# Gated-delta heads: decay rows by DMA a head ahead, key lengths from the Gram diagonal, output squares summed in one product

## The chip, the core and the metric

The kernel runs on one core of one Trainium2 chip. A core has five engines that run side by side and meet through semaphores: TensorE (PE in the profile; PEld is its weight load), VectorE (DVE), ScalarE (ACT), GpSimd (POOL) and SyncE (SP), which here only issues DMAs. SBUF is the on-chip memory with 128 partitions; PSUM (8 banks of 512 fp32 columns) is where TensorE writes. The metric is the device time of one execution in microseconds (us). The time before is 3914.38 us, the median of 3 runs (3914.11 to 3916.15).

## The reference, cut to what matters

The model is a chain of four blocks (attention, Hyena, gated DeltaNet with experts, short convolution with experts) on 512 tokens of width 1024, with 256 context tokens. The change touches only the DeltaNet mixer, which has 8 heads of width 128 and runs in two directions ("lanes"):

```python
qkv = silu(conv3_seq(p[..., :3 * d], conv_w))
q = l2norm(q) * HEAD_DIM ** -0.5        # l2norm(t) = t * rsqrt(sum(t * t) + 1e-6)
k = l2norm(k)
beta = sigmoid(...)                     # per token, direction, head
g = -exp(a_log) * softplus(a_in + dt_bias)
# gated_delta_scan, for each chunk, direction and head
gc = cumsum(g)
decay = exp(where(incl, gc[:, None] - gc[None, :], -inf))
lmat = where(i > j, (k * beta) @ k.T * decay, 0)
sol = triangular_solve(lmat, [v * beta, k * beta * exp(gc)])     # u, w
v_new = u - w @ s
s_next = s * exp(gc[-1]) + (k * exp(gc[-1] - gc)).T @ v_new
o = (q * exp(gc)) @ s + (q @ k.T * decay) @ v_new
# afterwards, per token and head
o = o * rsqrt(mean(o * o) + 1e-6) * onorm
y = (o * silu(z)) @ w_out
```

## The kernel before, in words

Every stage is a class with one method for each engine (`tensor`, `vector`, `scalar`, `gpsimd`, `sync`), and the order of the instructions on an engine is the order in which these methods issue them. Nothing is reordered; an engine that waits holds up all that stands behind it. `DeltaHeads` is one stage. It works in chunks of 128 tokens: `NTA` = 6 chunks (2 of context, 4 of latent tokens, `KEYS` = 768 columns), and for each of the 8 heads there are two parts.

*The inversion* (`tensor_invert`, `vector_invert`, `scalar_invert`) builds the inverse of the triangular matrix by doubling, in levels v = 1 to 6, for both lanes. A level is `masked(v, l)` on TensorE (L2498, 24 fp32 matmuls of 64x64 a lane), `keep_masked` on VectorE (L2838), `update(v, l)` on TensorE (L2519), `turn` on VectorE (L2844, a transpose from PSUM) and `keep_update` on ScalarE (L2698). The next level's `masked(v+1, l)` waits for `turn(v, l)`; `update(v, l)` waits for `keep_masked(v, l)` and for the `keep_update` of the level before. In the gaps TensorE does work that isn't part of the chain: it turns values and keys (L2442, L2448), sums the squares of the output of the head before (`tensor_sums`, L2457 and L2458, after level 3), spreads the root over the partitions (`tensor_spread`, L2465, after level 4), and computes the decay rows of the next head's lane 0 (`decays`, L2412, in level 5). An fp32 matmul leaves two MATMUL records; fp32r matmuls (L588) leave one.

*The scan* (`tensor_scan` and so on) walks through the 6 chunks of both lanes in steps 0 to 5. In each step TensorE multiplies the state by the keys (L2554, z), VectorE forms r (L2874), TensorE multiplies by the inverse (L2568, vn), ScalarE scales (L2742), VectorE scales again (L2884, vnd), TensorE makes the state's update (L2591, su) and VectorE adds it (L2893, s). Between these stand the projections of the *next* head (`project`, L588, three fp32r matmuls for each of 8 pieces), which are most of the work of the scan; ScalarE and VectorE convolve and activate the next head's q, k, v beside them. Step 0 ends with the decay rows of lane 1 of the next head (L2412), which wait until ScalarE has read those of lane 0 out of the same two PSUM banks (`grown`, L2645). Step 3 has the next head's Gram matrix k'k (L2423) and, behind it, the key lengths: ScalarE squares k into SBUF (L2633), and 6 matmuls against a column of ones sum the squares (L2427); VectorE waits for them (L2768) in `column_scales`.

The decay rows of a lane are a matrix whose every partition holds the cumulated g of all 768 tokens. `decay` on ScalarE makes of them exp(-relu(...)) in `L_M` (6 pieces by L2641, then L2644) and exp of the row in `L_KBG` (L2645). GpSimd halves them (L2220), and in `pool_head`, at the start of the inversion, reads `L_KBG` for the last columns (L2230), for q times decay (L2234), and makes q'k times decay (L2237); then it multiplies the gate by the head's output (L2245) and splits the next head's weights into a high and a low part (L582), each of which waits for ScalarE's copy of the high part (L577), which waits for the DMA of the weights.

SyncE issues four DMAs of 512 KB for the next head's weights as soon as the projections of the head before have ended (L2311). Counted semaphores: `COUNTED` gives names to certain counts of one semaphore.

The output of a head is normed in the inversion of the next head: ScalarE keeps it and squares it (L2678, L2682), TensorE sums the squares of o with those of q (times an epsilon), ScalarE takes the root (L2687), VectorE inverts it (L2822), TensorE spreads it, and VectorE multiplies (`norm_o`, L2829).

Of the kernel before, what the change touches and what calls it, by code (L numbers as in the profile page):

```python
# [1956 lines left out]
class DeltaGates:  # L1957
# [3 lines left out]
    def __init__(self, core):  # L1961
        self.c = core
        self.n = core.slab(k_slab(core.d["w_in_a_2"][0], 4 * D, 4 * D + 32))
        self.rows, self.rows0 = core.shared("table_in", 48)
# [168 lines left out]
class DeltaHeads(Stage):  # L2133
# [13 lines left out]
    PER = {"slab": 64, "full": 6, "centre": 5, "conv": 5, "silu": 6, "square": 1, "coef": 1, "nk": 1,  # L2147
           "osq": 1, "ostd": 1, "oroot": 1, "weighed": 1, "mixed": 1, "values_out": 1, "keys_out": 1, "qk": 1,
           "tri": 2, "cross": 2, "side": 1, "scored": 1, "a": 12, "a_in": 10, "a_out": 14, "x": 12,
           "upd": 12, "z": 10, "r": 10, "vn": 12, "vn_out": 13, "vnd": 12, "su": 12, "s": 12, "o": 1,  # L2150
           "begun": 7, "grew": 5, "onorm": 2}


    COUNTED = {"rows": ("begun", (1, 2)), "gram": ("begun", (3,)), "lens": ("begun", (4,)), "qkp": ("begun", (5,)),
               "turned": ("begun", (6, 7)), "flat": ("grew", (1, 3)), "grown": ("grew", (2, 4)), "eg": ("grew", (5,)),
               "osum": ("onorm", (1,)), "ospread": ("onorm", (2,))}

    def __init__(self, core, gates):
# [11 lines left out]
        self.sums, self.inverse, self.nk, self.root = (v(G_COL + 72 + 6 * i, n) for i, n in enumerate((NTA, NTA, NTA, NT)))  # L2170
# [33 lines left out]
    def gpsimd(self, pool):  # L2204
        for h in range(DHEADS):
            if h == 0:
                self.weights_low(pool, 0)
            self.halve_decays(pool, h)
            self.pool_head(pool, h)
            if h + 1 < DHEADS:  # L2210
                self.weights_low(pool, h + 1)
        self.weigh_o(pool, DHEADS - 1)
# [9 lines left out]
    def pool_head(self, pool, h):  # L2222

        if h:
            self.wait(pool, h - 1, "o", 1)
            self.wait(pool, h - 1, "s", 12)
# [12 lines left out]
        if h:  # L2239
            self.weigh_o(pool, h - 1)  # L2240

# [57 lines left out]
    def sync(self, sp):  # L2299
# [15 lines left out]
    def tensor(self, pe):  # L2315
        self.project(pe, 0, 1, range(KD))
# [5 lines left out]
        self.decays(pe, 0, 0)  # L2322
        self.decays(pe, 0, 1)
# [6 lines left out]
        self.tensor_spread(pe, DHEADS - 1)  # L2330

    def vector(self, dve):
# [18 lines left out]
        for h in range(DHEADS):  # L2351
            self.vector_invert(dve, h)
            self.vector_scan(dve, h)
        self.invert_root(dve, DHEADS - 1)
        self.norm_o(dve, DHEADS - 1)

    def scalar(self, act):
# [8 lines left out]
        self.square_k(act, 0)  # L2366
        self.centre(act, 0, 4)
        self.silu(act, 0, 3)
        self.silu(act, 0, 4)
        self.gate(act, 0)  # L2370
# [31 lines left out]
    def decays(self, pe, h, l):  # L2402

        c = self.c
        if l == 1:
            self.wait(pe, h, "grown", 1)
        elif h:
            self.wait(pe, h - 1, "keys_out", 1)
        else:
            pe.wait_ge(self.cols, 1)  # L2410
        for t in range(NTA):
            ins = pe.matmul(c.pair(6, KEYS)[:, P * t:P * t + P], self.g_all[:, t, l, h:h + 1].to_broadcast([P, P]),  # L2412
                            c.const(("cum_f", "cum_b")[l]), start=True, stop=True)
        ins.then_inc(self.s["begun"], 1)

    def gram(self, pe, h):
# [3 lines left out]
        self.wait(pe, h, "grown", 2)  # L2420
# [8 lines left out]
        ins.then_inc(self.s["begun"], 1)  # L2429

    def scores(self, pe, h):
        c = self.c
        self.wait(pe, h, "silu", 3)
        for t in range(NTC, NTA):
# [16 lines left out]
    def tensor_sums(self, pe, h):  # L2451

        c = self.c
        self.wait(pe, h, "osq", 1)
        for t in range(NT):
            out, cols = c.ps[:, 5, TC + t:TC + t + 1], slice(P * t, P * t + P)
            pe.matmul(out, self.o_sq[:, cols], c.const("one_over_p")[:, 0:1], start=True, stop=False)  # L2457
            ins = pe.matmul(out, self.q_sq[:, cols], c.eps(4), start=False, stop=True)  # L2458
        ins.then_inc(self.s["onorm"], 1)

    def tensor_spread(self, pe, h):
        c = self.c
        self.wait(pe, h, "oroot", 1)
        for t in range(NT):
            ins = pe.matmul(c.ps[:, 5, P * t:P * t + P], self.root[:, t:t + 1].to_broadcast([P, P]),  # L2465
                            c.const("ident"), start=True, stop=True)
        ins.then_inc(self.s["onorm"], 1)

    def tensor_invert(self, pe, h):
# [13 lines left out]
        def masked(v, l):  # L2483
# [5 lines left out]
            elif h and l == 0:  # L2489
                self.wait(pe, h - 1, "s", 12)  # L2490
# [38 lines left out]
        for v in range(2, LEVELS):  # L2529
# [4 lines left out]
            if v == 5 and h + 1 < DHEADS:  # L2534
                self.decays(pe, h + 1, 0)
# [4 lines left out]
            if v == 4 and h:  # L2540
                self.tensor_spread(pe, h - 1)

    def tensor_scan(self, pe, h):
        c, s = self.c, self.s
        more = h + 1 < DHEADS
        for step in range(NTA):
# [27 lines left out]
            for l in range(2):  # L2574
# [56 lines left out]
    def square_k(self, act, h):  # L2631
        act.drain()
# [1260 lines left out]
```

## Time and profile before

| | |
|---|---|
| time before, median of 3 | 3914.38 us |
| the profiled execution's own time | 3914.16 us |
| its span | 3912.3 us |
| TensorE busy | 3454.4 us (88% of the span) |
| VectorE busy | 1812.2 us (46%) |
| ScalarE busy | 1110.1 us (28%) |
| GpSimd busy | 420.5 us (11%) |
| `DeltaHeads`, first to last head's inversion | 1838 to 2370 us |

The lines of a timeline are: start, duration, engine, line of the kernel, operation, output and input by memory area, shape, count; in square brackets the idle time ahead of it on that engine and what ended it. Several like instructions in a row are merged. Matmuls overlap: the distance of two starts tells what one takes of the engine, not the duration.

### The profile page before, as it was taken

How to read it: one execution, taken by the hardware profiler on the slowest of the kernel's cores; microseconds unless marked ns; L12 is line 12 of the kernel's file. 1: busy time of each engine (PE TensorE's matmuls, PEld its weight loads, DVE VectorE, ACT ScalarE, POOL GpSimd, SP SyncE). 2: the span in 40 equal slices, each digit the busy share in tenths (PEclk: the TensorE clock that was granted, in tenths of full speed). 3: DMA queues.
4: the chain of work that ended last, by engine and by line, in shares of the span. 5: the costliest groups of instructions: out<-in, count | busy, mean ns of one | idle time of the engine just before them, and what ended most of it. 6: DMA issues, size and time to landing. Idle time of an engine off the chain costs nothing. (4 is left out here: it accounts for less than half of the span.)

```text
span 3912.3 us, 48632 instructions
## 1 busy us (share of the span) xinstructions
PE 3454.4 (88%) x18766; PEld 2323.2 (59%) x18766; DVE 1812.2 (46%) x2892; ACT 1110.1 (28%) x1849; POOL 420.5 (11%) x420
## 2 busy tenths in 40 slices
PE   8999899878999899887999998699987896998886
PEld 6756577754756677755888887444332674443332
DVE  6773777447865777435455445411111543111112
ACT  3051433223201433235544453211111322111112
POOL 1200000000300000002222320011111000111110
PEclk7999999988999899998999998799999897999998
DMA  6430355320622255310001001299997413999995
GB/s 220 172 109 22 107 173 172 114 108 22 247 108 86 86 172 172 109 26 23 23 23 45 23 23 46 98 414 392 424 415 300 167 45 118 417 402 415 398 391 218
DMA packets 222472, 689.48 MB, mean 176 GB/s; under 512 B 27699, under 2 KB 107699, under 8 KB 197076
## 3 DMA queue, kind: packets, MB, share of 16 engines
q1 hardware_dynamic: 192000, 648.17, 43.2%
q10 hardware_dynamic: 11572, 21.96, 1.5%
q0 software_dynamic: 18720, 16.84, 1.3%
q8 instruction: 126, 2.06, 0.2%
q14 instruction: 54, 0.44, 0.0%
HBM read 697.38 MB, written 40.89 MB: 189 GB/s over the span
## 5 line engine op out<-in xcount | busy, mean ns | idle before, releaser
L588 PE MATMUL psum<-work_rounded 128*128 128x512 f32 (+1 forms) x2224 | 815.4, 407 | 80.3 <-DVE work_rounded L582 30.3
L588 PE MATMUL psum<-work_rounded,ring_rounded 128*128 128x512 f32 (+1 forms) x1824 | 726.1, 398 | 0.0
L588 PEld LDWEIGHTS psum<-work_rounded 128*128 128x128 f32 x2224 | 428.7, 193 | 203.0 <-issue 93.9
L3434 PE MATMUL psum<-ring,fixed 128*64 128x512 f32 x1184 | 415.8, 657 | 96.1 <-DMA ring<-in_w 52.9
L577 ACT ACTIVATE work_rounded<-ring 128x1024 fp32r<-128x1024 f32 x204 | 214.6, 1057 | 950.7 <-PE psum L588 692.7
L588 PE MATMUL psum<-fixed_rounded,work_rounded 128*128 128x512 f32 (+1 forms) x1088 | 435.9, 401 | 0.0
L588 PEld LDWEIGHTS psum<-work_rounded,ring_rounded 128*128 128x128 f32 x1824 | 352.6, 193 | 81.1
L3589 DVE TENSOR_TENSOR work<-work,psum 64x512 f32<-64x512 f32 (+1 forms) x64 | 44.2, 691 | 701.9 <-ACT work L3519 547.3
L582 DVE TENSOR_TENSOR ring_rounded<-ring,work_rounded 128x1024 fp32r<-128x1024 f32 x189 | 230.1, 1220 | 283.0 <-ACT work_rounded L577 283.0
L3434 PEld LDWEIGHTS psum<-ring,fixed 128*64 128x64 f32 x1184 | 131.7, 150 | 333.0 <-issue 333.0
L362 DVE SCALAR_TENSOR_TENSOR work<-ring,fixed,work 128x512 f32<-128x512 f32 x364 | 300.5, 835 | 24.8 <-issue 0.9
L3434 PE MATMUL psum<-work,fixed 128*64 128x512 f32 x512 | 240.8, 626 | 0.0
L588 PE MATMUL psum<-ring_rounded 128*128 128x512 f32 (+1 forms) x768 | 238.5, 372 | 0.3 <-issue 0.3
L588 PEld LDWEIGHTS psum<-fixed_rounded,work_rounded 128*128 128x128 f32 x1088 | 210.7, 194 | 46.6 <-issue 2.6
L1274 DVE SCALAR_TENSOR_TENSOR work<-psum,fixed,work 128x511 f32<-128x511 f32 (+1 forms) x152 | 109.4, 720 | 142.1 <-ACT work L1356 108.2
L3519 ACT ACTIVATE work<-psum 64x512 f32<-64x512 f32 x53 | 31.3, 590 | 477.5 <-PE psum L3434 477.5
L3422 PE MATMUL psum<-ring,fixed 128*128 128x512 f32 x352 | 158.9, 611 | 1.8 <-DVE fixed L3581 1.8
L3343 POOL DMA_INDIRECT pair_rows<-work x66 | 66.7, 1011 | 809.0 <-DVE work L3605 663.8
L582 POOL TENSOR_TENSOR ring_rounded<-ring,ring_rounded 128x1024 fp32r<-128x1024 f32 x32 | 76.7, 2410 | 715.8 <-ACT ring_rounded L577 715.8
L588 PEld LDWEIGHTS psum<-ring_rounded 128*128 128x128 f32 x768 | 139.2, 189 | 21.1 <-issue 1.6
L582 POOL TENSOR_TENSOR ring_rounded<-ring,fixed_rounded 128x1024 fp32r<-128x1024 f32 x23 | 48.6, 2115 | 873.3 <-ACT fixed_rounded L577 873.3
L588 PE MATMUL psum<-fixed_rounded,ring_rounded 128*128 128x512 f32 (+1 forms) x384 | 137.0, 357 | 0.0
(396 smaller groups left out, 5159.7 us busy)
## 6 DMA issues: line engine op xcount, KB each, us to landing
ring<-in_w SPq DMA_DIRECT2D x128, 2048.0 KB, 17.3
work<-in_w SPq DMA_DIRECT2D x64, 2048.0 KB, 21.5
ring<-in_mod_w SPq DMA_DIRECT2D x24, 2048.0 KB, 9.0
ring<-in_ada_w SPq DMA_DIRECT2D x24, 2048.0 KB, 7.9
ring<-in_ffn_w_in SPq DMA_DIRECT2D x44, 1024.0 KB, 7.6
ring<-in_ffn_w_out SPq DMA_DIRECT2D x10, 2048.0 KB, 7.7
ring<-in_w_in_a SPq DMA_DIRECT2D x32, 512.0 KB, 6.6
ring<-in_hy_w_in SPq DMA_DIRECT2D x6, 2048.0 KB, 8.2
```

Of the source, the lines that this page charges most:

```text
L362: ins = dve.scalar_tensor_tensor(out=acc, in0=w[:, k, :], scalar=c.par(cond, k), in1=acc, op0=ALU.mult, op1=ALU.add)
L577: return act.activation(c.rounded(out), v, ACT.Copy)
L582: return eng.tensor_tensor(c.rounded(v), v, c.rounded(v_high), ALU.subtract)
L588: ins = pe.matmul(out, c.rounded(w), c.rounded(x), start=(start and i == 0), stop=(stop and i == 2))
L1274: dve.scalar_tensor_tensor(out=out[:, 1:n], in0=u[:, 0:n - 1], scalar=w0, in1=out[:, 1:n], op0=ALU.mult, op1=ALU.add)
L3343: pool.indirect_dma_start(self.c.d["pair_rows"], bass.IndirectOffsetOnAxis(ap=self.si[:, b:b + 1].bitcast(U32), axis=0), self.y_sb[:, b, : ...
L3422: ins = pe.matmul(c.ps[:, 2 + j, :], self.gt_sb[:, k, :], weights(o, j)[:, k, :], start=(k == 0), stop=(k == KD - 1))
L3434: ins = pe.matmul(c.ps[64 * j:64 * j + 64, 2, :], self.gt_sb[:, k, 0:64], weights(o, j)[:, k, :], start=(k == 0), stop=(k == KD - 1))
L3519: act.activation(self.s_sb[64:P, :].rearrange("p (k q) -> p k q", k=4), by_row(c.ps[0:64, 2, :]), ACT.Silu)\
L3589: dve.tensor_tensor(hh, s_sb, by_row(c.ps[rows, bank, :]), ALU.mult).then_inc(self.prod, 1)
```

## The change

- The decay rows come from memory. In head 0 the cumulated sums of all heads (96 columns) are transposed once on TensorE, copied by ScalarE and written to a table in DRAM (`keep_table`, DMA issued by ScalarE). From then on SyncE fetches both lanes' rows for the next head with two DMAs, broadcast to all partitions, straight into `L_KBG` of each lane, as soon as GpSimd has read the old ones (`scored`). ScalarE reads them there and writes the exp over them. TensorE's `decays` are left for head 0 only.
- The key lengths are the diagonal of the Gram matrix: VectorE multiplies its two 64-row halves by the identity and reduces. ScalarE's squares of k and TensorE's 6 products go.
- The output's squares: ScalarE scales q's square, GpSimd adds it to that of o (`add_q`, now the first thing in `pool_head`), and one 128x512 product against a matrix of 1/128 sums them. VectorE transposes the sums in 32x32 blocks (`turn_o`, level 4), ScalarE takes the root of 16 columns, and VectorE inverts and spreads it with a block transpose (`invert_root`, moved to level 5). `tensor_spread` goes.
- The state isn't updated any more in the last step of the scan, where nobody reads it.

```diff
     def pool_head(self, pool, h):
         if h:
+            self.add_q(pool, h - 1)
             self.wait(pool, h - 1, "o", 1)
-            self.wait(pool, h - 1, "s", 12)
+            self.wait(pool, h - 1, "s", 10)
...
+        if h == 0:
+            pool.wait_ge(self.gates.rows, self.gates.rows0 + 64)
...
+    def add_q(self, pool, h):
+        self.wait(pool, h, "osq", 1)
+        pool.tensor_tensor(self.o_sq, self.o_sq, self.q_sq, ALU.add).then_inc(self.s["ofull"], 1)
...
     def sync(self, sp):
...
+            if h == 0:
+                sp.wait_ge(self.gates.rows, self.gates.rows0 + 64)
+                continue
+            self.wait(sp, h - 1, "scored", 1)
+            for l in range(2):
+                rows = self.table.rearrange("(t l) (b n) -> l b t n", l=2, n=P)[l, h]
+                sp.dma_start(self.lane(l, L_KBG, NTA, P), rows.partition_broadcast(P)).then_inc(self.s["rows"], 16)
...
     def tensor(self, pe):
...
-        self.decays(pe, 0, 0)
-        self.decays(pe, 0, 1)
+        pe.wait_ge(self.cols, 1)
+        pe.transpose(c.ps[0:96, 3, 0:P], c.view(G_GC, 96), c.const("ident")).then_inc(self.gates.turned, 1)
+        self.first_decays(pe, 0)
+        self.first_decays(pe, 1)
...
     def gram(self, pe, h):
         self.wait(pe, h, "silu", 2)
-        self.wait(pe, h, "grown", 2)
+        if h == 0:
+            self.wait(pe, 0, "grown", 2)
         for t in range(NTA):
             ...
-        self.wait(pe, h, "square", 1)
-        for t in range(NTA):
-            ins = pe.matmul(c.ps[:, 7, TC + t:TC + t + 1], self.lane(0, L_L, NTA, P)[:, t, :],
-                            c.const("ones")[:, 0:1], start=True, stop=True)
...
     def tensor_sums(self, pe, h):
-        self.wait(pe, h, "osq", 1)
-        for t in range(NT):
-            out, cols = c.ps[:, 5, TC + t:TC + t + 1], slice(P * t, P * t + P)
-            pe.matmul(out, self.o_sq[:, cols], c.const("one_over_p")[:, 0:1], start=True, stop=False)
-            ins = pe.matmul(out, self.q_sq[:, cols], c.eps(4), start=False, stop=True)
-    def tensor_spread(self, pe, h):
...
+        self.wait(pe, h, "ofull", 1)
+        pe.matmul(c.ps[:, 5, :], c.const("one_over_p"), self.o_sq, start=True, stop=True).then_inc(self.s["osum"], 1)
...
     def tensor_invert(self, pe, h):
...
-            if v == 5 and h + 1 < DHEADS:
-                self.decays(pe, h + 1, 0)
...
-            if v == 4 and h:
-                self.tensor_spread(pe, h - 1)
     def tensor_scan(self, pe, h):
...
-                self.wait(pe, h, "vnd", i + 1)
-                pe.matmul(c.ps[:, 2 * l, 2 * P:3 * P], self.kt[:, t, :], self.st(l, 3), start=True, stop=True)\
-                    .then_inc(s["su"], 1)
+                if step < NTA - 1:
+                    self.wait(pe, h, "vnd", i + 1)
+                    pe.matmul(c.ps[:, 2 * l, 2 * P:3 * P], self.kt[:, t, :], self.st(l, 3), start=True, stop=True)\
+                        .then_inc(s["su"], 1)
...
-                if step == 0:
-                    self.decays(pe, h + 1, 1)
...
+    def keep_table(self, act):
+        act.wait_ge(self.gates.turned, 3)
+        staged = self.lane(0, L_QD, P)[0:96, :]
+        act.activation(staged, self.c.ps[0:96, 3, 0:P], ACT.Copy).then_inc(self.cols, 1)
+        act.wait_ge(self.cols, 2)
+        act.dma_start(self.table.rearrange("a (b n) -> (a b) n", n=P), staged).then_inc(self.gates.rows, 16)
...
     def decay(self, act, h, l):
-        m, rows = self.lane(l, L_M, NTA, P), c.pair(6, KEYS).rearrange("p (t n) -> p t n", n=P)
-        self.wait(act, h, "rows", l + 1)
+        m, rows = self.lane(l, L_M, NTA, P), self.lane(l, L_KBG, NTA, P)
+        if h:
+            self.wait(act, h - 1, "rows", 32)
+        else:
+            act.wait_ge(self.gates.turned, 4 + l)
+            rows = c.pair(6, KEYS).rearrange("p (t n) -> p t n", n=P)
...
     def column_scales(self, dve, h):
-        self.wait(dve, h, "lens", 1)
-        dve.tensor_scalar(self.sums, self.c.ps[:, 7, TC:TC + NTA], RMS_EPS, None, ALU.add)
+        self.wait(dve, h, "gram", 1)
+        g, diagonal = self.c.pair(6, KEYS).rearrange("p (t n) -> p t n", n=P), self.compact(0, L_L)
+        for half in self.halves():
+            dve.tensor_tensor(diagonal[half], g[half, :, half], self.ident()[half], ALU.mult)
+        dve.drain()
+        dve.tensor_reduce(self.sums, diagonal, AX.X, ALU.add)
+        dve.drain()
+        dve.tensor_scalar(self.sums, self.sums, RMS_EPS, None, ALU.add)
...
+    def turn_o(self, dve, h):
+        self.wait(dve, h, "osum", 1)
+        dve.transpose(self.o_sq, self.c.ps[:, 5, :])
+        dve.drain().then_inc(self.s["oturn"], 1)
     def invert_root(self, dve, h):
         self.wait(dve, h, "ostd", 1)
         dve.reciprocal(self.root, self.root)
-        dve.drain().then_inc(self.s["oroot"], 1)
+        dve.drain()
+        spread(dve, self.o_sq, self.root)
+        dve.drain()
     def norm_o(self, dve, h):
-        self.wait(dve, h, "ospread", 1)
         self.wait(dve, h, "weighed", 1)
-        dve.scalar_tensor_tensor(..., in1=self.c.ps[:, 5, :], ...)
+        dve.scalar_tensor_tensor(..., in1=self.o_sq, ...)
     def vector_invert(self, dve, h):
         for v in range(1, WHOLE + 1):
...
+            if v == 4 and h:
+                self.turn_o(dve, h - 1)
+            if v == WHOLE and h:
+                self.invert_root(dve, h - 1)
             for l in range(2):
                 turn(v, l)
...
-            if v == 4 and h:
-                self.invert_root(dve, h - 1)
     def vector_scan(self, dve, h):
...
+                if step == NTA - 1:
+                    continue
```

The `continue` stands in both inner loops of `vector_scan` (vnd and s). ScalarE's `deviate_o` (the root) moves from level 3 to level 4, ahead of `square_q`, and `square_o` waits for the norm of the head before.

## Rows read from the trace of the kernel before

**Rows 1.** Window of one head: length, busy us (instructions) of each engine, PEclk.
```profile
2064.91:2141.09 76.18, 72.58 (x896) 64.66 (x897) 39.32 (x90) 36.55 (x78) 21.04 (x16) 1.00 0.12 29
```
**Rows 2.** Timeline of TensorE in the scan: end of step 0, then steps 3 and 4.
```profile
2102.13 1.60 PE L2412 MATMUL psum<-fixed,work 128*128 128x128 f32 x12 [0.29 <-ACT work L2645]
2103.57 0.61 PE L2554 MATMUL psum<-work 128*128 128x128 f32 x4
...
2119.17 1.40 PE L2427 MATMUL psum<-fixed,work 128*128 128x1 f32 x12
2120.43 0.36 PE L588 MATMUL psum<-ring_rounded 128*128 128x256 f32 x1
...
2125.84 0.75 PE L2568 MATMUL psum<-work 128*128 128x128 f32 x4
```
**Rows 3.** Timeline of ScalarE, first instruction of steps 1 and 2.
```profile
2105.16 0.62 ACT L2742 ACTIVATE work<-psum,work 128x128 f32<-128x128 f32 x2 [3.08 <-PE psum L2568]
...
2110.68 0.62 ACT L2742 ACTIVATE work<-psum,work 128x128 f32<-128x128 f32 x2 [1.06 <-PE psum L2568]
```
**Rows 4.** Timeline of VectorE, steps 3 and 4 of the same scan.
```profile
2123.39 0.16 DVE L2768 TENSOR_SCALAR work<-psum 128x6 f32<-128x6 f32 x1
...
2124.24 1.12 DVE L2782 TENSOR_TENSOR work<-work,psum 64x384 f32<-64x384 f32 x2 [0.19 <-issue]
2125.43 0.61 DVE L2874 SCALAR_TENSOR_TENSOR work<-psum,work 128x128 f32<-128x128 f32 x2
```
**Rows 5.** Groups of VectorE by form: busy us, mean ns of one, then idle.
```profile
L1113 DVE TENSOR_REDUCE work<-psum 128x1 f32<-128x768 f32 x32 | 29.1, 952 | 12.3 <-PE psum L1070 12.3
...
L512 DVE STREAM_TRANSPOSE work<-psum 128x512 f32<-128x512 f32 x11 | 7.9, 716 | 37.5 <-PE psum L478 37.5
```
**Rows 6.** Timelines at a change of heads: VectorE, TensorE and GpSimd.
```profile
1908.39 0.75 DVE L1277 SCALAR_TENSOR_TENSOR work<-psum,fixed,work 128x511 f32<-128x511 f32 x1
...
1910.26 0.55 DVE L2793 TENSOR_TENSOR work<-work 128x384 f32<-128x384 f32 x1
...
1912.85 1.15 DVE L2795 TENSOR_TENSOR work<-work 128x384 f32<-128x384 f32 x1
...
1914.73 0.86 PE L2480 MATMUL psum<-work,fixed 64*64 64x384 f32 x4 [0.86 <-DVEq L2798]
...
1912.76 0.82 POOL L2231 COPY work<-work 128x768 f32<-128x768 f32 x1
```
**Rows 7.** Timelines of VectorE and GpSimd in levels 3 and 4.
```profile
2079.80 1.41 DVE L2815 COPY work<-work 128x6 f32<-128x6 f32 x2
...
2082.02 1.26 DVE L2838 TENSOR_TENSOR work<-psum,work 128x384 f32<-128x384 f32 x2 [0.65 <-PE psum L2498]
...
2076.45 4.67 POOL L582 TENSOR_TENSOR ring_rounded<-ring,ring_rounded 128x1024 fp32r<-128x1024 f32 x2 [3.31 <-ACT ring_rounded L577]
```
**Rows 8.** Timeline of TensorE, the sums, then levels 4 and 5.
```profile
2079.18 0.38 PE L2457 MATMUL psum<-fixed,work 128*128 128x1 f32 x2
...
2081.06 1.61 PE L2498 MATMUL psum<-work 64*64 64x64 f32 x48
...
2086.11 1.61 PE L2498 MATMUL psum<-work 64*64 64x64 f32 x48
```
**Rows 9.** The DMA issues: KB of each, median us to landing.
```profile
ring<-in_w_in_a SPq DMA_DIRECT2D x32, 512.0 KB, 6.6
```
**Rows 10.** Windows with PEclk: the first head's opening, then two in the experts.
```profile
1813.00:1843.60 30.60, 16.91 (x122) 14.49 (x122) 8.86 (x17) 10.47 (x22) 9.59 (x9) 0.61 0.28 70
...
2813.00:2816.40 3.40, 3.40 (x10) 1.20 (x8) 0.00 (x0) 0.00 (x0) 1.24 (x2) 0.50 1.00 423
...
2864.20:2891.00 26.80, 21.84 (x109) 8.75 (x105) 4.13 (x6) 4.76 (x8) 3.66 (x6) 1.00 1.01 425
```
**Rows 11.** Timeline of TensorE, two matmuls of the experts behind idle time.
```profile
2811.83 0.61 PE L3434 MATMUL psum<-ring,fixed 128*64 128x512 f32 x1 [2.00 <-DMA work<-in_w]
...
2875.75 0.61 PE L3434 MATMUL psum<-ring,fixed 128*64 128x512 f32 x1 [2.00 <-DMA work<-in_w]
```

More of the change, by code:

```diff
@@ L1963, in __init__ @@
         self.n = core.slab(k_slab(core.d["w_in_a_2"][0], 4 * D, 4 * D + 32))
-        self.rows, self.rows0 = core.shared("table_in", 48)
+        self.rows, self.rows0 = core.shared("table_in", 64)
         (self.full, self.sigmoid, self.shifted, self.soft, self.gate, self.turned) = (
@@ L2133 @@
 class DeltaHeads(Stage):
-    PER = {"slab": 64, "full": 6, "centre": 5, "conv": 5, "silu": 6, "square": 1, "coef": 1, "nk": 1,
-           "osq": 1, "ostd": 1, "oroot": 1, "weighed": 1, "mixed": 1, "values_out": 1, "keys_out": 1, "qk": 1,
+    PER = {"slab": 64, "full": 6, "centre": 5, "conv": 5, "silu": 6, "coef": 1, "nk": 1, "rows": 32,
+           "osq": 1, "ofull": 1, "oturn": 1, "ostd": 1, "weighed": 1, "mixed": 1, "values_out": 1, "keys_out": 1, "qk": 1,
            "tri": 2, "cross": 2, "side": 1, "scored": 1, "a": 12, "a_in": 10, "a_out": 14, "x": 12,
[L2150 to L2156, printed above, removed]
+           "upd": 12, "z": 10, "r": 10, "vn": 12, "vn_out": 13, "vnd": 10, "su": 10, "s": 10, "o": 1,
+           "begun": 4, "grew": 5, "osum": 1}
+    COUNTED = {"gram": ("begun", (1,)), "qkp": ("begun", (2,)), "turned": ("begun", (3, 4)),
+               "flat": ("grew", (1, 3)), "grown": ("grew", (2, 4)), "eg": ("grew", (5,))}
     def __init__(self, core, gates):
@@ L2169, in __init__ @@
         self.kd, self.gl, self.eg, self.bg, self.coef, self.ahead = (v(G_COL + 12 * i, 2, NTA) for i in range(6))
-        self.sums, self.inverse, self.nk, self.root = (v(G_COL + 72 + 6 * i, n) for i, n in enumerate((NTA, NTA, NTA, NT)))
+        self.sums, self.inverse, self.nk, self.root = (v(G_COL + 72 + 6 * i, n) for i, n in enumerate((NTA, NTA, NTA, T // 32)))
+        self.table = core.d["h_rows"][0:2 * NTA, :]
         self.taps = v(PAR0 + PAR["conv_a0"][0], 3, 3, DHEADS)
@@ L2211, in gpsimd @@
                 self.weights_low(pool, h + 1)
+        self.add_q(pool, DHEADS - 1)
         self.weigh_o(pool, DHEADS - 1)
@@ L2353, in vector @@
             self.vector_scan(dve, h)
+        self.turn_o(dve, DHEADS - 1)
         self.invert_root(dve, DHEADS - 1)
@@ L2369, in scalar @@
         self.silu(act, 0, 4)
+        self.keep_table(act)
         self.gate(act, 0)
@@ L2400, in project, with first_decays @@
             ins.then_inc(self.s["full"], 1)
-    def decays(self, pe, h, l):
+    def first_decays(self, pe, l):
         c = self.c
[L2405 to L2410, printed above, removed]
+        if l:
+            self.wait(pe, 0, "grown", 1)
         for t in range(NTA):
-            ins = pe.matmul(c.pair(6, KEYS)[:, P * t:P * t + P], self.g_all[:, t, l, h:h + 1].to_broadcast([P, P]),
+            ins = pe.matmul(c.pair(6, KEYS)[:, P * t:P * t + P], self.g_all[:, t, l, 0:1].to_broadcast([P, P]),
                             c.const(("cum_f", "cum_b")[l]), start=True, stop=True)
-        ins.then_inc(self.s["begun"], 1)
+        ins.then_inc(self.gates.turned, 1)
     def gram(self, pe, h):
@@ L2433, in scores @@
         self.wait(pe, h, "silu", 3)
+        if h == 0:
+            pe.wait_ge(self.cols, 2)
         for t in range(NTC, NTA):
@@ L2489, in masked @@
             elif h and l == 0:
-                self.wait(pe, h - 1, "s", 12)
+                self.wait(pe, h - 1, "s", 10)
             if v > WHOLE:
@@ L2629, in convolve @@
             .then_inc(self.s["conv"], 1)
-    def square_k(self, act, h):
-        act.drain()
-        act.activation(self.lane(0, L_L, KEYS), self.k, ACT.Square).then_inc(self.s["square"], 1)
+    def keep_table(self, act):
[4 more added lines that the diff above has]
+        act.dma_start(self.table.rearrange("a (b n) -> (a b) n", n=P), staged).then_inc(self.gates.rows, 16)
     def decay(self, act, h, l):
         c, s = self.c, self.s
-        m, rows = self.lane(l, L_M, NTA, P), c.pair(6, KEYS).rearrange("p (t n) -> p t n", n=P)
-        self.wait(act, h, "rows", l + 1)
+        m, rows = self.lane(l, L_M, NTA, P), self.lane(l, L_KBG, NTA, P)
[4 more added lines that the diff above has]
+            rows = c.pair(6, KEYS).rearrange("p (t n) -> p t n", n=P)
         for t in range(NTA):
@@ L2644, in decay @@
         act.activation(flat, flat, ACT.Exp, scale=-1.0).then_inc(s["grew"], 1)
-        act.activation(self.lane(l, L_KBG, KEYS), c.pair(6, KEYS), ACT.Exp).then_inc(s["grew"], 1)
+        act.activation(self.lane(l, L_KBG, NTA, P), rows, ACT.Exp).then_inc(s["grew"], 1)
     def growth(self, act, h):
@@ L2681, in square_o @@
         self.wait(act, h, "vn_out", 13)
+        if h:
+            self.wait(act, h - 1, "mixed", 1)
         act.activation(self.o_sq, self.o, ACT.Square).then_inc(self.s["osq"], 1)
@@ L2685, in deviate_o @@
         c = self.c
-        self.wait(act, h, "osum", 1)
-        act.activation(self.root, c.ps[:, 5, TC:TC + NT], ACT.Sqrt, bias=c.eps(5)).then_inc(self.s["ostd"], 1)
+        self.wait(act, h, "oturn", 1)
+        act.activation(self.root, fine(self.o_sq), ACT.Sqrt, bias=c.eps(5)).then_inc(self.s["ostd"], 1)
     def scalar_invert(self, act, h):
@@ L2758, in scalar_scan @@
                     self.silu(act, h + 1, step - 1)
-                if step == 2:
-                    self.square_k(act, h + 1)
         self.keep_o(act, h)
@@ L2822, in invert_root @@
         dve.reciprocal(self.root, self.root)
[L2823 removed]
+        dve.drain()
+        spread(dve, self.o_sq, self.root)
+        dve.drain()
     def norm_o(self, dve, h):
[L2827 removed]
         self.wait(dve, h, "weighed", 1)
[L2829 removed]
+        dve.scalar_tensor_tensor(out=self.mixed(h), in0=self.mixed(h), scalar=self.c.par("onorm_a"), in1=self.o_sq,
                                  op0=ALU.mult, op1=ALU.mult).then_inc(self.s["mixed"], 1)
@@ L2890, in vector_scan @@
                 t = self.order[l][step]
+                if step == NTA - 1:
+                    continue
                 self.wait(dve, h, "su", i + 1)
```

16 lines of the change are left out of this document (3 added, 13 removed).

## The prediction

> **What bounds the kernel now.** I read the page first for the shares (TensorE 88%), then cut the stage into heads by the first matmul of each inversion. A head takes 76.2 us, and TensorE is busy for 72.6 of them at the full clock, VectorE for 39, ScalarE for 37, GpSimd for 21 [rows 1]. So a head is bound by TensorE's queue, and idle time is only 3.6 us. What leaves that queue is worth its spacing, unless the work beside it (VectorE's in the main) isn't ready that early. So every removed block is followed in the timelines: when could what stands behind it start, and what would it then wait for? I follow the head from 2064.9 to 2141.1 us, and one change of heads at 1912 us.
>
> **The scan: lane 1's decay rows.** The twelve records of L2412 start at 2102.13 after 0.29 of idle, and step 1's first matmul at 2103.57 [rows 2]: 1.44 + 0.29, and some 0.2 by which the projection's last matmul overlaps its successor where none waits. Step 1 can start near 2101.7: **1.9 us** gained (1.73 at least). Its cover is ScalarE, which still makes the decays, now out of SBUF: it waited 3.08 us for TensorE in step 1 and 1.06 in step 2 [rows 3]; of the first 1.9 go, and the second moves along with TensorE. Both stay above zero, so nothing is late next; reading SBUF instead of PSUM may cost it some 0.3 us a lane, which still fits.
>
> **The scan: key lengths.** TensorE loses L2427, from 2119.17 to 2120.43: 1.26 us [rows 2]. VectorE gains two products of 64x384 out of PSUM, 1.12 us by L2782, which has their shape [rows 4]; a reduction of 384 columns; and gaps of 0.1 to 0.2. No row has that reduction: L1113 takes 0.95 for 768 columns [rows 5], which bounds it above, and half of that, 0.48, is near the bottom; I take 0.55, since the fixed part doesn't halve. Together +1.85 (1.7 to 2.3). Before, column scales, weighing and r follow without a gap from 2123.39 on; lane 0's half of r (0.61 for two) ends near 2125.75, and the matmul that wants it starts at 2125.84 [rows 2, 4]. So VectorE is already just on the path here. With TensorE 1.26 earlier and VectorE's block 1.85 longer, r comes 0.6 later than before: this edit **costs 0.6 us** a head (0.4 to 1.0), and TensorE idles some 1.9 us in step 4.
>
> **The change of heads.** VectorE does not wait for the last state update: it starts the next inverse after the convolution, which ends at 1909.14, and not at 1910.26 [rows 6]: 1.06 earlier. The add L2795 took 1.15 while GpSimd copied (1912.76 to 1913.58), 0.56 elsewhere; GpSimd's copies now come behind `add_q`, which waits for ScalarE's square, so this 0.59 should go too. TensorE itself loses four records (0.45). The second lane's first matmul at 1914.73 waited 0.86 for VectorE; it gains **1.6 us**, the sum of 1.06 and 0.59, near what TensorE's queue then allows.
>
> **The inversion to level 4.** GpSimd gets 1.27 more work (an add like L2245) and starts it some 1.7 us later, since it waits for the square and no more for the output; it ends about 3 us later, still ahead of the weights, which arrive 11 us after the last projection and reach GpSimd at 2076.45 [rows 7]. They arrive only as much earlier as the projections end: 0.45. And the weights' split holds VectorE: the small copy L2815 is issued at 2079.80, takes 1.41 for two of 128x6, and ends with GpSimd's second split at 2081.12 [rows 7]; five of seven heads show it. So L2838 of level 4, at 2082.02, can move to about 2080.95 (2081.12 - 0.45 + 0.28 for the small operations): **1.07 us** for all up to here, in place of 2.2 that the change of heads and the sums would give. The sums: L2457/L2458 take 1.88 of spacing (2079.18 to 2081.06) [rows 8]; one fp32 product of 512 columns is as wide as two records at 0.43, so about 1.0. This 0.9 is inside what the copy swallows. If GpSimd slips behind its longer queue, up to 0.5 of the 1.07 is lost.
> The Trainium skill, "SBUF — State Buffer", section "SBUF: two separate sides", says that VectorE and GpSimd share a port pair under an exclusive lock, which a VectorE operation with two SBUF inputs or in a two-port mode asks for. L2815 and L2795 agree. By the rule the moved GpSimd block can also hit VectorE's cross products (L2808) by up to 1.3 us; the time would be the same, as these are ahead of the copy that waits anyway.
>
> **Levels 4 and 5.** Before: from L2838 at 2082.02 to `masked(5)` at 2086.11, 4.09 us, as the spread stands between, an idle wait for the inverted root and eight records [rows 7, 8]. After: two masks 1.23, `turn_o` 0.72 [rows 5] and a drain of 0.1, the first turn 0.6 and a hop of 0.05: 2.75. Gain **1.35 us**. In level 5 the twelve records of lane 0 go, as long as lane 1's [rows 2], **1.5 us**, 0.1 of which may turn into a wait for the mask. `invert_root` (a reciprocal of 0.13, a transpose like L512's [rows 5], drains, 1.1 in all) lies under `update(5)`, which takes 2.6 us; without that cover it costs 1.1. The root on ScalarE moves to where its input is ready, and needs no new table. Together 1.07 + 1.35 + 1.42 = 3.84; less 0.3 for GpSimd's queue I take **3.5 us** for an inversion including the change of heads.
>
> **The rest.** SyncE: in front of the row DMAs it waits for `scored`, early in the inversion; the next wait (`full`) is a scan later, so nothing is held. The DMAs (393 KB each in 512-byte pieces) have from about 2077 to 2097 to land; 512 KB take 6.6 us [rows 9]. First head: a transpose, a copy and a DMA issue go ahead of ScalarE's chain (+0.5 to 1), the lengths (2.6 at the low clock) go, 1.85 is added on VectorE: 0 ± 1. Last head: the scan's end -0.45; then GpSimd's add, one product, two transposes in place of sixteen and eight records: 0 ± 0.7.
>
> **Sum.** Inversions of heads 1 to 6: 6 x 3.5 = 21.0. Head 7 had no decay rows of a further head: 3.5 - 1.5 = 2.0. Head 0 has only those: 1.5. Scans of heads 0 to 6: 7 x (1.9 - 0.6) = 9.1. Last scan 0.45. Together 34.0 us. The profiled execution took 3914.16 us around its span of 3912.3, and the median is 3914.38; 3914.2 - 34.0 = **3880 us**.
>
> **Rivals.**
> (a) *VectorE's copy doesn't hold*, as in the two heads whose weights came early. Then 2.2 in place of 1.07 (and no 0.3 off) before level 4: 1.3 more a head over six or seven, 3872. For it: two of seven heads. Against: the copy is now issued earlier, further inside the split.
> (b) *The clock falls for a moment in step 4.* The new idle stretch is 1.9 us. In the experts, 2.0 us of idle were once followed by 3.4 us at 1.2 GHz, and once by no fall in 27 us [rows 10, 11]. Each fall costs half of 3.4, 1.7 us; in all seven scans 12 us, 3892. The Trainium skill, "TensorE: Matmul & The Clock Gate", section "HAM oscillation — how this bites in real kernels", names such a fall at each repeat of a wait as a trap; the trace has both outcomes for one length of idle time, 2.00 us.
> (c) *Slower: the clock stays down after that idle time.* The first head's opening, where TensorE is busy for only 16.9 of 30.6 us, ran at 0.61 of the clock [rows 10]. A fall of 13.7 us in each scan would cost 6.8 x 7 = 48 us and give 3928. It decides above some 9.7 us of low clock a scan (34/7 x 2). For it: only that stretch, with far more idle time, showed so long a fall. Against: dense projections stand on both sides.
> (d) *The diagonal is dearer, or its operations are held too*: +1 us more a scan, 3887.
> (e) *The rows come late*, and ScalarE blocks in step 0: that needs a landing 20 us after issue; it makes it slower from 25 on.
>
> **Chances.** Forecast 0.57; (a) 0.15; (b) 0.14; (c) 0.03; (d) 0.09; (e) 0.02. The range goes from 3866 ((a) with the sums and first head at their good ends) to 3894 ((b)). What a measurement of this kernel can tell from no change is about 0.2%, 8 us, so the gain is four times that. Faster by over 0.2%: 0.94 (all but (c), (e) and a little for what I don't see); within: 0.02; slower: 0.04.
>
> **What would show it.** Heads of about 71.4 us between first matmuls (76.2 - 3.5 - 1.3). L2412's successor only in the first head. TensorE's idle time in step 4 at about 1.9 us and released by r. The small copies still long, ending with GpSimd's second split, and L2838 of level 4 right behind. `masked(5)` 2.7 us after it. No `rows` wait on ScalarE. The forecast is wrong if the heads lose under 4 us (then look at the clock and at the diagonal), or over 6 (the copies no longer wait).

## The result, and the profile after

The changed kernel takes **3938.16 us** in the median (3928.9 to 3945.68, 5 runs), the kernel before 3914.38 (3910.09 to 3917.4, 5 runs): ratio 1.0061, 95% interval 1.005 to 1.0072. It is 24 us slower, where 34 us of gain were forecast. The profiled execution took 3938.16 us around its span of 3936.3.

The windows of the kernel after (length, busy us and instructions of TensorE, its weight loads, VectorE, ScalarE, GpSimd, then PEclk, DMA share, GB/s): the head that answers to [rows 1], then two stretches of it.
```profile
2076.90:2158.60 81.70, 71.31 (x836) 62.97 (x837) 41.49 (x91) 36.28 (x77) 21.99 (x15) 0.92 0.15 37
...
2087.00:2101.50 14.50, 10.04 (x250) 8.51 (x250) 9.01 (x19) 8.01 (x13) 10.06 (x5) 1.00 0.23 54
2103.50:2115.50 12.00, 12.00 (x124) 11.32 (x125) 1.86 (x3) 3.88 (x8) 0.00 (x0) 0.50 0.00 1
```
TensorE has 60 instructions fewer than before, yet the head is 5.5 us longer. Its idle time is 10.4 us in place of 3.6, and for 12 us at the end of the inversion and the start of the scan it runs at 0.50, half its clock, where all of that head had 1.00 before. TensorE's timeline in level 5, and SyncE's of the same head, show what precedes it:
```profile
2093.76 1.61 PE L2520 MATMUL psum<-work 64*64 64x64 f32 x48
2095.78 1.61 PE L2499 MATMUL psum<-work 64*64 64x64 f32 x48 [0.41 <-DVE work L2859]
2097.36 0.33 PE L2518 MATMUL psum<-work 64*64 64x64 f32 x2
2103.47 0.48 PE L2520 MATMUL psum<-work 64*64 64x64 f32 x4 [5.79 <-issue]
```
```profile
2076.65 4.56 SPq L2320 DMA_DIRECT2D ring<-in_w_in_a  x4
2086.22 1.54 SPq L2328 DMA_DIRECT2D work<-h_rows  x2
```
In the middle of a block of matmuls whose inputs are there, TensorE stops for 5.79 us, and "issue" says that nothing in the profile released it. Each of the seven inversions with row DMAs has such a stop: 4.3, 10.0, 8.7, 5.8, 5.1, 7.5 and 10.7 us, 52 in all. The last head, which has no row DMAs, has none. The waits of TensorE over these heads (in total, times, longest):
```profile
PE psum L2499 <- issue: 26.9, 3, 10.7
PE psum L2520 <- issue: 25.2, 4, 10.0
PE psum L2499 <- DVE work L2859: 12.3, 15, 0.9
PE psum L2565 <- DVE work L2891: 11.8, 7, 1.7
```
The row DMAs need 13.8 us to land:
```profile
work<-h_rows SPq DMA_DIRECT2D x14, 384.0 KB, 13.8
```
512 KB of weights take 6.6 [rows 9]. From 2087.0 to 2101.5 they move 54 GB/s with a DMA share of 0.23, so the engines aren't busy, but slow. The trace has one more kind of packet: pieces of 16,384 bytes on a queue that the page of the profile calls "instruction" (a second queue of that name has pieces of 8,192 bytes at most). Its packets start at 2082.34 and 2086.43, then there is none until 2101.17, and TensorE goes on at 2103.47.

**Theory 1:** while the row DMAs are in flight, the next 16 KB of TensorE's instructions aren't fetched, and TensorE, which in the inversion asks for a packet every 4 to 7 us, runs dry; the clock falls after the stop. **Theory 2:** the stops come from how the changed program lies in memory. **Theory 3** (my rival (c)): the clock falls because of the new idle time in step 4.

### The profile page after: what moved, and what is told of

Same layout as the page of the kernel before. It is cut to its first block and busy times, and to the rows that moved or that the text cites. A ratio compares the mean times of both kernels' runs of the same rounds, so it can differ in the third digit from the quotient of the medians.

```text
span 3936.3 us, 47732 instructions
## 1 busy us (share of the span) xinstructions
PE 3411.9 (87%) x18295; PEld 2280.4 (58%) x18295; DVE 1830.5 (47%) x2900; ACT 1107.0 (28%) x1842; POOL 428.2 (11%) x428
## 5 line engine op out<-in xcount | busy, mean ns | idle before, releaser
L3364 POOL DMA_INDIRECT pair_rows<-work x66 | 66.8, 1013 | 808.3 <-DVE work L3626 663.0
L588 PEld LDWEIGHTS psum<-ring_rounded 128*128 128x128 f32 x768 | 139.8, 190 | 21.2 <-issue 1.6
```

Source lines behind the costliest of these rows:

```text
L588: ins = pe.matmul(out, c.rounded(w), c.rounded(x), start=(start and i == 0), stop=(stop and i == 2))
L3364: pool.indirect_dma_start(self.c.d["pair_rows"], bass.IndirectOffsetOnAxis(ap=self.si[:, b:b + 1].bitcast(U32), axis=0), self.y_sb[:, b, : ...
```

## The experiments

Times are medians of 4 to 10 runs, each beside 7 to 13 runs of the kernel before on the same chip (medians 3913.2 to 3913.9).

**The row DMAs alone, in the kernel before**
```
+            self.wait(sp, h - 1, "scored", 1)
+            for l in range(2):
+                rows = table.rearrange("(t l) (b n) -> l b t n", l=2, n=P)[l, h]
+                sp.dma_start(self.lane(l, L_KBG, NTA, P), rows.partition_broadcast(P))...   # overwritten unused
...
+        if h:
+            self.wait(act, h - 1, "rows_in", 32)       # ScalarE, ahead of the decays
```


> The kernel before, and nothing of the change but its row DMAs: two broadcasts of six 512-byte rows to 128 partitions a head, at the place and into the buffer that the change uses; ScalarE waits for them where it makes the decays, and what they bring is overwritten unused. Theory 1 (while these DMAs are in flight TensorE's instructions aren't fetched, and it runs dry in the inversion): seven stalls of 5 to 10 us that nothing releases, each followed by some 10 us at half clock, none of the instruction queue's packets between issue and landing; the whole cost of the change beside its forecast, 3938 - 3880 = 58 us, comes back here: about 3972, at least 3950. Theory 2 (the stalls come from how the changed program lies in memory) and theory 3 (the clock falls after the new idle time in step 4): no stalls, 3914 within 4.

Measured: 3991.3 us, ratio 1.0197 (1.018 to 1.0214): 77 us slower. TensorE's waits:
```profile
PE psum L2529 <- issue: 38.8, 7, 10.4
PE psum L2467 <- issue: 11.2, 1, 11.2
PE psum L2508 <- issue: 8.6, 1, 8.6
```
Seven of these stops have 5.4 to 11.2 us, 57.6 together; the other 20 us go with the clock, which is at half for 89 us in these heads. Two DMAs whose data nothing uses, with the waits for them, make the effect in the kernel before, and make it larger than the 58 us that I had expected. Theory 3 falls, as step 4 is here as it was before. Theory 2 gave no stops here; that the few added instructions shift the program in memory is ruled out further below, where the same instructions with another source make no stop.

**The change without the row DMAs**
```
-            for l in range(2): ... sp.dma_start(self.lane(l, L_KBG, NTA, P), ...)
+            if v == 5 and h + 1 < DHEADS: self.decays(pe, h + 1, 0)
+            if step == 0: self.decays(pe, h + 1, 1)
```


> The change without its row DMAs: decay rows by TensorE's twelve products a head as before, key lengths from the diagonal, squares in one product, last state updates skipped. Theory 1: no stall; from the forecast 3880 the decay rows come back, 7 x (1.9 + 1.5) = 24 us: about 3904 (3898 to 3910), faster than before. Theory 2: stalls stay, or lie elsewhere: over 3920. Theory 3: TensorE still idles 1.7 us in step 4, so the low clock stays at those places: over 3925.

Measured: 3899.03 us, ratio 0.9966 (0.9953 to 0.9978), as expected, and no stop. Step 4's idle time of 1.68 us is there in all seven scans, and no fall of the clock follows it; the only 3.4 us at half clock in these heads come in an inversion, 0.8 us behind a wait of 1.93 us for VectorE. One of the six other heads:
```profile
1911.40:1985.30 73.90, 68.93 (x858) 60.31 (x859) 41.48 (x91) 35.61 (x77) 21.96 (x15) 1.00 0.12 30
```

**The same bytes in fewer pieces**
```
-        act.dma_start(self.table.rearrange("a (b n) -> (a b) n", n=P), staged)
+        for t in range(NTA): act.dma_start(table[t], staged[16 * t:16 * t + 16])       # HBM order l b t n
-                rows = self.table.rearrange("(t l) (b n) -> l b t n", l=2, n=P)[l, h]
+                rows = self.table.rearrange("a n -> (a n)").rearrange("(l b t n) -> l b t n", ...)[l, h]
```


> The change, its table in HBM laid out so that the six rows of a head and lane lie side by side: a partition's share is one piece of 3 KB and not six of 512 bytes, 128 pieces a lane in place of 768; the same bytes from the same place, at the same time. Theory 1a (each piece costs time in the queue, and the count of pieces holds the fetch): in flight for some 3 us in place of 14, stalls under 2 us, 3880 to 3892. Theory 1b (128 reads of one spot of HBM are what is slow, by bytes): flight and stalls as in the change, 3938 within 6. Theory 2: stalls stay, 3938.

Measured: **3871.4 us**, ratio 0.9892 (0.9876 to 0.9909), 9 us below the 3880 to 3892 of theory 1a, since the forecast that it stands on had the change's gain too small (see "Why the prediction was wrong"). No stop is left. Its row DMAs, TensorE's waits in the heads, and one head:
```profile
work<-h_rows SPq DMA_DIRECT2D x14, 384.0 KB, 4.2
```
```profile
PE psum L2499 <- DVE work L2861: 16.3, 22, 0.9
PE psum L2565 <- DVE work L2893: 11.8, 7, 1.7
...
PE psum L2481 <- issue: 1.8, 7, 0.3
...
PE psum L2520 <- issue: 0.3, 1, 0.3
```
```profile
2048.20:2118.70 70.50, 65.79 (x834) 57.66 (x835) 41.43 (x91) 36.13 (x77) 21.99 (x15) 1.00 0.16 42
```
The pieces of 3 KB pass at 82 to 88 a us at their densest, and those of 512 bytes in the kernel after at 45 to 90, but for some 500 of the 1536 that pass within 3 us around the middle of the flight. (One lane alone has no such burst, and I can't explain it.) So the price isn't by the byte. That it is by the piece, the like rates don't show: 85 pieces of 3 KB are 261 GB/s, near the 280 to 350 of the weights' 512-byte pieces (550 to 690 a us), so they may be held by their bytes, where the rows' 512-byte pieces move 23 to 46 GB/s outside the burst. With 3-KB pieces the DMA share is 0.67 in this window, against 0.23 in the kernel after:
```profile
2059.20:2062.50 3.30, 3.30 (x89) 3.00 (x83) 1.70 (x3) 2.02 (x5) 2.94 (x2) 1.00 0.67 192
```
What is slow, then, are 512-byte pieces; but why 85 a us, when the weights' pieces of the same size pass at 550 to 690?

**The row DMAs in the scan**
```
+            self.wait(sp, h - 1, "a_out", 14)      # the inversion's end, before the two DMAs
-                if step == 0: self.decay(act, h + 1, 0)      -      if step == 1: self.decay(act, h + 1, 1)
+                if step == 2: self.decay(act, h + 1, 0)      +      if step == 3: self.decay(act, h + 1, 1)
```


> The change with its row DMAs issued at the end of the inversion, in flight during the scan, where TensorE uses its instructions up more slowly (512 columns each, not 64); ScalarE makes the decays in steps 2 and 3 and not in 0 and 1. Theory 1: the gap in the instruction queue moves with them, TensorE has instructions in stock for it or stalls for under 2 us: 3880 to 3895 (the upper end if the decays now come late for the weighing in step 4). Theory 2: stalls stay where they are, 3938. Theory 3: 3938, or more.

Measured: 3884.58 us, ratio 0.9925 (0.9909 to 0.9942). The DMAs are as slow (14.3 us), but no stop of over 1 us is left: in the scans of the kernel before, TensorE's packets come only every 12 to 27 us. The 13 us to the kernel with 3-KB pieces lie in the scan: 43.3 to 44.7 us in place of 42.6, and a part of them in a longer wait for r in step 4 (the rest I didn't trace):
```profile
PE psum L2566 <- DVE work L2893: 15.6, 7, 2.3
```

**One place or many: the same pieces from places of their own**
```
-                rows = table.rearrange("(t l) (b n) -> l b t n", l=2, n=P)[l, h]
+                rows = w[0:NTA * P, at:at + P].rearrange("(t p) n -> p t n", p=P)
```


> The kernel before with two extra DMAs a head as in e1_rows_only (same place in the program, same buffer, 1536 pieces of 512 bytes, brought in and overwritten unused), but each piece is read from a place of its own, out of the input weights, in place of 128 partitions reading the same six pieces. Theory 1b (128 reads of one place in HBM are what is slow): in flight for some 3 us (1536 pieces at the 600 a us of the weights' own DMAs), no stall, 3914 to 3920. Theory 1a (the count of pieces): as e1_rows_only, 14 us in flight and 3991.

Measured: 3913.01 us, ratio 1.0002 (0.9992 to 1.0011), landing in 4.5 us, no stop:
```profile
work<-in_w_in_a SPq DMA_DIRECT2D x14, 384.0 KB, 4.5
```
As many pieces of the same size, to the same places in SBUF, with the same waits. So neither their count nor their size alone makes them slow, but that 128 partitions read the same six.

**Half of it**

Its edit: `for l in range(1)` around the row DMA of the first experiment.

> e1_rows_only with the row DMA of lane 0 alone: half the pieces, from the same places. Theory 1 with a stock of instructions: TensorE holds what was fetched before, so the stall is the time in flight less what the stock lasts; 7 us in flight in place of 14 leaves stalls of 0 to 3 us where e1_rows_only had 5 to 11: 3914 to 3935, less than half of its 77 us. A rival in which the stall is proportional to the pieces would give half: 3952.

Measured: 3955.73 us, ratio 1.0108 (1.0091 to 1.0125), a miss: 43 us, over half of 77. Landing takes 11.3 us, not 7: the weights' last pieces come first, and then the rows pass for 9 us:
```profile
work<-h_rows SPq DMA_DIRECT2D x7, 384.0 KB, 11.3
```
The stock of instructions, as the cause, holds all the same. Packets on the instruction queue, and TensorE's stops:
```
kernel                packet starts     next      gap    TensorE stops at   goes on   after the packet's start
after                 2086.43           2101.17   14.7   2097.68            2103.47   2.3
row DMAs alone        2016.39           2032.08   15.7   2023.83            2034.23   2.2
one lane alone        1997.07           2007.75   10.7   2004.57            2009.95   2.2
small, one place      1998.20           2005.07    6.9   2005.63            2007.41   2.3
```
In these kernels the stops of 1.5 us or more that nothing releases all end 2.15 to 3.05 us after the start of a packet, nearly all 2.2 to 2.4. In the table each stop begins 7.4 to 11.3 us after the start of the last packet that came in time, so a stock lasts about that long. The counts settle whose packets these are: in the three kernels with two DMAs or one, from the end of each stop to the end of the next TensorE and its weight load leave 1536, 1792 or 2048 records (to within 1), for 6, 7 or 8 packets, 256 for each. From the start of the last packet in time to a stop of 4 us or more they leave 347 to 553, so the stock is about two packets. TensorE stops because it has run out of instructions; what was wrong is my size for the half.

**Eight copies of the table, and the control to it**
```
+                for copy in range(8):
+                    part = c.d["h_rows"][16 * copy:16 * copy + 2 * NTA]          # control: [0:2 * NTA]
+                    sp.dma_start(self.lane(l, L_KBG, NTA, P)[16 * copy:16 * copy + 16], ...partition_broadcast(16))
```


> e1_rows_only with the table in HBM eight times, each copy read by 16 partitions: the same pieces, still one source for many partitions, but an eighth of the reads at each place (16 small DMAs in place of 2). Theory 1b, in which reads of one place queue up: the pieces pass at several times the 85 a us, 2 to 5 us in flight, stalls under 2 us, 3914 to 3925. Rival (it is the repeated source in a DMA's pattern that is slow, whatever the place): 14 us in flight, 3991.

> e9_eight_copies, all sixteen small DMAs a head reading the first of the eight copies: small DMAs, one place. e9 took away the stalls although its pieces still needed some 13 us, so one of its two differences from e1_rows_only did it. If it is the place (reads of one place fill what the instruction's own read must pass): the stalls are back, 3950 to 3991. If it is the size of the DMA (16 issues with gaps, between which a fetch gets in): no stalls, 3914 to 3920.

Measured: with eight copies 3916.16 us, ratio 1.0003 (0.9993 to 1.0013); with the same sixteen small DMAs from one copy 3944.22, ratio 1.0081 (1.006 to 1.0102). The DMA issues of the first and of the second:
```profile
work<-h_rows SPq DMA_DIRECT2D x112, 48.0 KB, 3.9
```
```profile
work<-h_rows SPq DMA_DIRECT2D x112, 48.0 KB, 6.9
```
The place matters by itself: 28 us between two kernels that differ only in it. But small DMAs help too: 31 us of loss in place of 77, with stops of 1.2 to 3.4 us (with eight copies one of 1.5 is left), and packets of instructions now come through in between. So my two answers for the control were too sharp: both differences count. My flight of 2 to 5 us for the eight copies was wrong: SyncE needs 8.7 us to issue sixteen DMAs, so their pieces were still spread over some 12 us; that they let the fetch pass is what counts.

**The diagonal, and a version that beats both.** Three kernels on top of the one with 3-KB pieces: key lengths by TensorE as before; VectorE's weighing of lane 0 moved behind r of step 4; both.
```
             if more and step == 3:
                 self.column_scales(dve, h + 1)
-                self.weigh(dve, h + 1, 0)
...
+            if more and step == 4: self.weigh(dve, h + 1, 0)     # behind r, ahead of scale_columns
```


> e3_rows_3kb with the key lengths as before: ScalarE squares k, TensorE's six one-column products follow the Gram product, VectorE adds. My step on the diagonal (it costs 0.4 to 0.6 us a scan, as VectorE's block grows by more than TensorE's queue loses): 3871.4 - 7 x 0.5 = 3868 (3866 to 3870). Rival (the lengths' wait for ScalarE's square and for TensorE matters as much, so the diagonal gains): 3873 to 3878.

> e3_rows_3kb with one move in VectorE's queue: lane 0's weighing of the Gram matrix goes from the end of step 3 behind r of step 4, so that r isn't queued behind it. If VectorE's block is what makes TensorE idle for 1.7 us in step 4: that idle time falls to some 0.1, and 7 x 1.2 to 1.7 us are gained: 3860 to 3863. Rival (what comes behind r, the weighted v and the state update of step 4, is late in its place): 3868 to 3872.

> e8_weigh_later with the key lengths on ScalarE and TensorE again, as in e7_lengths_on_pe. If the diagonal cost something only because r was queued behind it, then with r in front TensorE's 1.26 us a scan are a net gain of the diagonal: this kernel is slower than e8_weigh_later by 7 x 1.26 less its last 0.3 us of idle: some 7 us, 3870 to 3874. Rival (the diagonal costs 0.5 a scan wherever r stands): 3861.

Measured: 3869.57 us (ratio 0.9886, 0.9869 to 0.9902), **3864.65** (0.9877, 0.986 to 0.9893) and 3868.46 (0.9892, 0.9875 to 0.9908). The first is as expected, the second some 2 us above its range and the third as much below. The intervals overlap, so I go by heads, which repeat to 0.1 us in nearly all cases: 70.5 with 3-KB pieces, then 70.0, 69.3 and 69.9. The wait for r in the second of the three:
```profile
PE psum L2565 <- DVE work L2893: 2.9, 7, 0.4
```
It was 11.8 before. So the diagonal costs 0.5 us a head while r is queued behind VectorE's block, and brings 0.6 once it isn't (I had expected 1.0). The move is what the trace of step 4 asked for, and that kernel is 1.2% faster than the one before.

## Why the prediction was wrong

**The step that failed** is in "The rest": "The DMAs (393 KB each in 512-byte pieces) have from about 2077 to 2097 to land ... nothing is held". I asked who waits for the rows (ScalarE, rival (e), which indeed didn't come), and priced their flight by the weights' row [rows 9]. They are slow in a way that row didn't show, and what they held was no semaphore's waiter but TensorE's supply of instructions: 13.8 us to land, and seven stops of 52.1 us together, which the sum has at nothing. The kernel after and the one with 3-KB pieces differ by 66.8 us: 52.1 are stops, the other 15 go with half clock, of which the kernel after has 65 us in seven stretches. The clock falls during the stop, 1.5 to 5.1 us after it begins, so 28 of the 65 us lie inside the stops and cost nothing more. The 36.5 behind them would have taken half at full clock, 18 us; and TensorE's waits for VectorE in L2499 shrink from 16.3 us to 12.3, which by this estimate leaves 14 of the 15.

The Trainium skill, "Runtime: NRT & Kernel Launch", section "Instruction fetch mechanics", says that an engine's instructions stream in by 16 KiB blocks over a DMA queue of its own while the present block runs, and that this is hidden since the engine issues more slowly than blocks arrive. The packets of 16,384 bytes agree; the 52 us of stops don't agree with the hiding, and the measurement decides. The Trainium skill, "DMA: Bandwidth & Descriptors", section "Queues, rings and completion order", says that each of the 16 engines serves its rings in turn and changes only after some 9 to 17 descriptors, at most 64. An estimate by that section of the Trainium skill: 1536 pieces over 16 engines at 85 a us are 5.3 a us for each, so a turn takes 2 to 3 us, and 12 at its longest. That sixteen small DMAs let packets through fits. What doesn't fit a turn of 2 to 3 us is the kernel after: the next packet starts 11.3 to 16.8 us behind the issue of the row DMAs (leaving aside one that starts 0.2 us behind it), and in five of seven heads only 0.1 to 0.9 us before the last piece of the rows is through. So by what way the fetch waits stays open; no run tested it.

**The other steps**, from the kernels without stops:

*The scan: lane 1's decay rows* (1.9 forecast). From the first L2565 to the next head the scan takes 42.63 us with 3-KB pieces, and 44.56 with TensorE's decay rows: 1.93. ScalarE's cover was right; its timeline in the kernel after answers to [rows 3]:
```profile
2116.85 1.85 ACT L2644 ACTIVATE work<-work 128x128 f32<-128x128 f32 x6
...
2122.57 0.62 ACT L2747 ACTIVATE work<-psum,work 128x128 f32<-128x128 f32 x2 [0.94 <-PE psum L2565]
```
*The scan: key lengths* (0.6 cost, 1.9 idle). TensorE idles 1.68 us in step 4, released by r:
```profile
2143.75 0.75 PE L2565 MATMUL psum<-work 128*128 128x128 f32 x4 [1.68 <-DVE work L2891]
```
Less the 1.26 saved that is 0.42 of cost, and taking the diagonal out gave 0.5. Rival (d) fell.

*The change of heads and the inversion to level 4.* The second lane's first matmuls wait no more (0.86 in [rows 6]), as TensorE's timeline with 3-KB pieces shows:
```profile
2048.86 0.89 PE L2499 MATMUL psum<-work 64*64 64x64 f32 x24
2049.56 0.84 PE L2481 MATMUL psum<-work,fixed 64*64 64x384 f32 x4
```
And the small copy does end with GpSimd's second split, level 4 right behind. VectorE and GpSimd of the kernel after, beside [rows 7]:
```profile
2091.75 1.31 DVE L2824 COPY work<-work 128x6 f32<-128x6 f32 x2
...
2093.14 1.26 DVE L2853 TENSOR_TENSOR work<-psum,work 128x384 f32<-128x384 f32 x2
2094.32 0.71 DVE L2831 STREAM_TRANSPOSE work<-psum 128x512 f32<-128x512 f32 x1
2095.14 1.05 DVE L2859 STREAM_TRANSPOSE work<-psum 128x384 f32<-128x384 f32 x2
```
```profile
2088.28 4.68 POOL L582 TENSOR_TENSOR ring_rounded<-ring,ring_rounded 128x1024 fp32r<-128x1024 f32 x2 [0.60 <-ACT ring_rounded L577]
```
Rival (a) fell.

*Levels 4 and 5* (1.35 and 1.42). `masked(5)` starts 2.64 us behind L2853, 2.75 forecast. From the first matmul of an inversion to `masked(5)`, 21.2 us became 18.9 (2.3; 2.4 forecast with the part to level 4), and from there to the scan 10.5 became 9.0 (1.5).

Without stops a head loses 5.7 us (76.25 to 70.5), where 4.8 were forecast: 0.3 that I took off for GpSimd weren't needed, 0.45 of the four last records I let the copy swallow though they shorten the scan, and the diagonal was 0.2 cheaper. With pieces of 3 KB the change brings 43 us, not 34; that 3871 lies inside my range is owed to its width, as the sum was 9 us short. The forecast missed one term, of the other sign and larger.

**Rivals (b) and (c)**, the clock. With 3-KB pieces no idle stretch of 1.68 us in step 4 was followed by a fall, nor in the kernel after or the change without row DMAs, seven in each; with the rows in the scan one of seven, of 2.05 us, was, by the stretch of 3.4 us at half clock in this window, and six of 2.24 to 2.27 weren't:
```profile
2253.20:2256.60 3.40, 3.40 (x11) 2.82 (x11) 3.25 (x5) 2.86 (x6) 1.58 (x1) 0.50 0.00 0
```
Long falls did come, up to rival (c)'s size (3.4 to 13.7 us a head), but in stops of 4 to 11 us and not in step 4.

## What to carry to other kernels

A transfer that nobody waits for can still cost time: look for what else travels with it, and for waits that end with "issue" while it is in flight. Where many partitions read the same few pieces of HBM, let each read as few and as long pieces as the layout allows, spread them over copies, or put the DMA beside long matmuls instead of many short ones. And when work is taken from a queue, ask what stands in front of the result it waits for next: moving one block behind r was worth 1.2 us a head, over twice the 0.5 that the diagonal cost.

## What the hardware showed that I had not expected

- Reads of one place in HBM by 128 partitions, in 512-byte pieces, pass at 45 to 90 a us for most of their flight; the same count from places of their own at 450 to 620. In pieces of 3 KB they pass at 82 to 88 a us, six times the bytes.
- While such reads are in flight, no packet of instructions starts for 11.3 to 16.8 us from their issue (kernel after), though the engines' share is only 0.23 in the window shown.
- TensorE and its weight load leave 256 records for each packet. In the inversion (64-column matmuls) TensorE lives 7 to 11 us on its stock, and starts again mostly 2.2 to 2.4 us after the next packet starts; in the scan it fetches a packet only every 12 to 27 us.
- The granted clock falls 1.5 to 5.1 us into a stop of 4.3 to 10.7 us, and is at half for 3.4 to 13.7 us (kernel after).
